# Experts of seven products: the products in another order, the gather issued an expert ahead, and the weight slots reloaded in another order

## The chip, the cores and the metric

The kernel runs on one core of a Trainium2 chip. The metric is the device time of one execution in microseconds, as a median over runs; the profile is of one further execution. Engines: PE (TensorE), DVE (VectorE), ACT (ScalarE), POOL (GpSimd), SP (SyncE, which here only issues DMAs).

## The reference, cut to what matters

A first block (attention, gated linear attention, RWKV branch) is followed by two layers, each a mixer and then a mixture of 16 experts. The change touches the two mixtures alone:

```python
def expert_choice_moe(x, w_router, w_gate_up, w_down):      # S = 1024, D = FF = 1024, 16 experts
    cap = CAPACITY_FACTOR * S // N_EXPERTS                  # 128 tokens an expert
    aff = jax.nn.softmax((x @ w_router), axis=-1)
    gates, idx = lax.top_k(jnp.swapaxes(aff, 1, 2), cap)
    xs = x[bi, idx]                                         # gather 128 rows
    g, u = jnp.split(jnp.einsum('becd,edf->becf', xs, w_gate_up), 2, axis=-1)
    out = jnp.einsum('becf,efd->becd', jax.nn.silu(g) * u, w_down) * gates[..., None]
    return jnp.zeros_like(x).at[bi, idx].add(out)           # scatter-add
```

An expert has 12 MB of fp32 weights (8 MB gate and up, 4 MB down), so the two mixtures read 400 MB of weights.

## The kernel before

`moe` handles the experts one after the other. Every engine has one instruction queue, worked in the order in which the program writes it, and semaphores tie the queues. The weights go through `ring`, 24 slots of 512 KB: slots 0 to 15 take gate and up, 16 to 23 take down. SP reloads a slot for the next expert when its readers are done.

Experts 0 to 2 and 15 multiply plainly. Experts 3 to 14 (`SEVEN`) compute gate and up, seen as a 2 x 2 block product (tokens halved by 64, rows of the weights halved, gate against up), by seven block products in the manner of Strassen and Winograd. Each quarter of the weights is 4 slots. In the names below a quarter is q0 to q3 (slots 0-3, 4-7, 8-11, 12-15).

- Sums of weights, on DVE, each over 128 x 1024 values and each in four parts j: t1 (in place in q1) = q1 - q0 (`sum_first`), t2 = q2 - t1 (`sum_second`), t3 = t2 - q0 (`sum_third`), t4 = t2 - q3, in place in t2 (`sum_fourth`).
- Sums of tokens, on POOL: s1, s3, s2, s4 in this order (`sum_tokens`, L4207 to L4212).
- Products, on PE, 16 matmul instructions each (L3631): 11 (q0), s2t2, s3t3, s1t1 (slots of q1), 22t4, 12b21 (q3), s4b22 (q2). `made` counts them in the order of `PRODUCTS`.
- Joins, on DVE, from PSUM banks (`join`): u2, u3, c22, u4, c21, 11, c12. The second half of the hidden row is sigmoid(c21) * c21 * c22, the first sigmoid(11) * 11 * c12; the sigmoids are ACT's.

PE's order for expert e is: s2t2, s3t3, s1t1, 22t4 | transposes of the next expert's gathered tokens (`turn_tokens`, L3604) | 12b21 | transposes of the second hidden half (`turn_half(e, 0)`, L3691) | s4b22 | first half of the next expert's product 11 | transposes of the first hidden half (`turn_half(e, 1)`) | second half of the next 11 | the down product, 32 matmul instructions (L3618). The last thing before `turn_half(e, 1)` is s4b22 -> c12 (L4067) -> product with the hidden half (L4070).

DVE's order is: u2, t4 parts 0 and 1, u3, t4 parts 2 and 3, c22, u4, c21 (L4049), c21 * c22 (L4051), product with the sigmoid (L4054), t1 parts 0 and 1 of the next expert (L4004), join 11 (L4059), t1 parts 2 and 3, product (L4065), c12, product (L4070), and then t2 and t3 of the next expert (L4012, L4016).

POOL's order is: gather of expert e+1 (L4195, an indirect DMA into `xg`, allowed once the tokens of e are transposed), token sums of e+1, scatter-add of e (L4232, after ACT has scaled the output). So the gather of e+1 stands behind the scatter of e-1.

SP's order of loads for e+1 is: slots 0-3 when t3 (all parts) and product 11 of e are made; slots 20-23 of e itself, four late slots; slots 4-7 after s1t1; 12-15 after 12b21; 8-11 after s4b22; 16-19 as the down product frees them.

Of the kernel before, what the change touches and what calls it, by code (L numbers as in the profile page):

```python
# [13 lines left out]
P = 128  # L14
# [3389 lines left out]
def moe(k, c, ps, io, layer, X, rows, out, sb):  # L3404
# [7 lines left out]
    with stage(k, sb) as st:  # L3412
# [39 lines left out]
        PRODUCTS = ("11", "s2t2", "s3t3", "s1t1", "22t4", "12b21", "s4b22")  # L3452
        JOINS = ("u2", "u3", "22", "u4", "21", "11", "12")
# [37 lines left out]
        quarter = lambda q, j: ring[:, 4 * q + j, :, :].rearrange("p x c -> p (x c)")  # L3491
        t2 = lambda j: X[:, j, :]
        t3 = lambda j: X[:, half_rows + j, :]

# [14 lines left out]
        def sync(sp):  # L3509
            def load(e, i):  # L3510
                sp.dma_start(ring[:, i, :, :], slab(e, i)).then_inc(*landed[i].up(16))

            for e in range(SEVEN[0] + 1):
                for i in range(SLABS if e < SEVEN[0] else 20):
                    if e:
                        sp.wait_ge(used.sem, used_at(e - 1, i + 1))
                    load(e, i)
                if e == 1:
                    sp.wait_ge(logits.sem, NT)
                    sp.dma_start(g, io["ln_ffn_g_2"][layer].partition_broadcast(P)).then_inc(*ln_in.up(16))  # L3520
                    sp.dma_start(b, io["ln_ffn_b_2"][layer].partition_broadcast(P)).then_inc(*ln_in.up(16))
            for e in SEVEN:
                sp.wait_ge(w_summed.sem, w_summed_at(e, "t3_3"))
                sp.wait_ge(made.sem, made_at(e, "11"))
                for i in range(4):
                    load(e + 1, i)
                for i in range(20, SLABS):
                    sp.wait_ge(used.sem, used_at(e - 1, i + 1))
                    load(e, i)
                sp.wait_ge(made.sem, made_at(e, "s1t1"))  # L3530
                for i in range(4, 8):
                    load(e + 1, i)
# [3 lines left out]
                sp.wait_ge(made.sem, made_at(e, "s4b22"))  # L3536
                for i in range(8, 12):
                    load(e + 1, i)
                for i in range(16, 20):
                    sp.wait_ge(used.sem, used_at(e, i + 1))  # L3540
                    load(e + 1, i)
            for i in range(20, SLABS):
                sp.wait_ge(used.sem, used_at(NE - 2, i + 1))
                load(NE - 1, i)
# [15 lines left out]
        def tensor(pe):  # L3560
# [54 lines left out]
            def multiply(e, i, lhsT, banks):  # L3615
                pe.wait_ge(landed[i].sem, 16 * (e + 1))
# [24 lines left out]
            def weight(q):  # L3641
                return lambda j: quarter(q, j)

            def landed_all(e, q):
                for j in range(4):
                    pe.wait_ge(landed[4 * q + j].sem, 16 * (e + 1))

            def first_product(e, lo, hi):

                if lo == 0:  # L3650
# [3 lines left out]
                    if e > SEVEN[0]:  # L3654
                        pe.wait_ge(joined.sem, joined_at(e - 1, "u3"))
                m = product(first_bank(e), x_quarter(e, 0, 0), weight(0), (lo, hi))
# [3 lines left out]
            def four_products(e):  # L3660
# [3 lines left out]
                pe.wait_ge(x_summed.sem, x_summed_at(e, "s2"))  # L3664
# [3 lines left out]
                product(ps[3], summed(0), weight(1)).then_inc(*made.up())  # L3668
# [3 lines left out]

            def fifth_product(e):

                pe.wait_ge(kept.sem, e - SEVEN[0] + 1)
                landed_all(e, 3)
                product(first_bank(e), x_quarter(e, 0, 1), weight(3)).then_inc(*made.up())

            def last_product(e):

                pe.wait_ge(joined.sem, joined_at(e, "u4"))
                pe.wait_ge(x_summed.sem, x_summed_at(e, "s4"))
                landed_all(e, 2)
                product(ps[3], summed(3), weight(2)).then_inc(*made.up())

            def turn_half(e, i):
# [3 lines left out]
                for b in range(4):  # L3690
                    m = pe.transpose(ps[4 + i][:, b * P:(b + 1) * P], hid[:, 512 * (1 - i) + b * P:512 * (1 - i) + (b + 1) * P],  # L3691
# [69 lines left out]
        def scalar(ac):  # L3761
# [43 lines left out]
            def keep_first(e):  # L3805

                if e > SEVEN[0]:
                    ac.wait_ge(acted.sem, 4 * e - 1)
# [3 lines left out]
            def sigmoid_half(e, i):  # L3812
                if i == 0:
                    ac.wait_ge(joined.sem, joined_at(e, "21"))
                    ac.activation(hid[:, 512:1024], c21, ACT.Sigmoid).then_inc(*sig.up())
                else:
                    ac.wait_ge(joined.sem, joined_at(e, "11"))
                    ac.activation(hid[:, 0:512], first_kept[:, :], ACT.Sigmoid).then_inc(*sig.up())

            def copy_half(e, i):  # L3820

                ac.wait_ge(h_turned.sem, 2 * e + i + 1)
                ac.activation(hs[:, :].rearrange("p (s b r t) -> p s b r t", s=2, b=4, r=2)[:, :, :, 1 - i, :],
# [28 lines left out]
            for e in range(NE - 1):  # L3852
                if e in SEVEN:
                    copy_tokens(e + 1)
                    for i in range(2):
                        sigmoid_half(e, i)
                        copy_half(e, i)
# [87 lines left out]
        def vector(ve):  # L3945
# [51 lines left out]
            def sum_first(e, j):  # L3997
# [4 lines left out]
                for q in (0, 1):  # L4002
                    ve.wait_ge(landed[4 * q + j].sem, 16 * (e + 1))
                ve.tensor_tensor(quarter(1, j), quarter(1, j), quarter(0, j), ALU.subtract).then_inc(*w_summed.up())  # L4004

            def sum_second(e, j):

                ve.wait_ge(landed[8 + j].sem, 16 * (e + 1))
# [3 lines left out]
                ve.tensor_tensor(t2(j), quarter(2, j), quarter(1, j), ALU.subtract).then_inc(*w_summed.up())  # L4012

            def sum_third(e, j):
                ve.wait_ge(w_summed.sem, w_summed_at(e, f"t2_{j}"))
                ve.tensor_tensor(t3(j), t2(j), quarter(0, j), ALU.subtract).then_inc(*w_summed.up())  # L4016

            def sum_fourth(e, j):

                ve.wait_ge(made.sem, made_at(e, "s2t2"))  # L4020
                ve.wait_ge(landed[12 + j].sem, 16 * (e + 1))
                ve.tensor_tensor(t2(j), t2(j), quarter(3, j), ALU.subtract).then_inc(*w_summed.up())  # L4022
# [8 lines left out]
            def join(e):  # L4031
# [11 lines left out]
                ve.wait_ge(made.sem, made_at(e, "s1t1"))  # L4043
                ve.wait_ge(joined.sem, joined_at(e, "u3"))
                ve.tensor_tensor(c22[:, :], ps[3][:, :], u3[:, :], ALU.add).then_inc(*joined.up())
                ve.wait_ge(made.sem, made_at(e, "s1t1"))
                ve.tensor_tensor(u2[:, :], ps[3][:, :], u2[:, :], ALU.add).then_inc(*joined.up())
# [4 lines left out]
                ve.wait_ge(sig.sem, 2 * e + 1)  # L4052
                ve.wait_ge(*acted.now())
                ve.tensor_tensor(hid[:, 512:1024], hid[:, 512:1024], c22[:, :], ALU.mult).then_inc(*acted.up())  # L4054
                if e + 1 in SEVEN:
                    sum_first(e + 1, 0)
                    sum_first(e + 1, 1)
                ve.wait_ge(made.sem, made_at(e, "12b21"))
                ve.tensor_tensor(first_kept[:, :], first_bank(e)[:, :], first_kept[:, :],  # L4059
                                 ALU.add).then_inc(*joined.up())  # L4060
                if e + 1 in SEVEN:
                    sum_first(e + 1, 2)
                    sum_first(e + 1, 3)
                ve.wait_ge(sig.sem, 2 * e + 2)
                ve.tensor_tensor(hid[:, 0:512], hid[:, 0:512], first_kept[:, :], ALU.mult).then_inc(*acted.up())  # L4065
                ve.wait_ge(made.sem, made_at(e, "s4b22"))
                ve.tensor_tensor(c12, ps[3][:, :], u2[:, :], ALU.add).then_inc(*joined.up())  # L4067
                ve.wait_ge(joined.sem, joined_at(e, "12"))
                ve.wait_ge(*acted.now())
                ve.tensor_tensor(hid[:, 0:512], hid[:, 0:512], c12, ALU.mult).then_inc(*acted.up())  # L4070
                if e + 1 in SEVEN:
# [121 lines left out]
        def gpsimd(gp):  # L4193
# [4 lines left out]
            def sum_tokens(e):  # L4198
# [6 lines left out]
                if e > SEVEN[0]:  # L4205
                    gp.wait_ge(made.sem, made_at(e - 1, "s4b22"))
# [160 lines left out]
```

## Time and profile before

| what | us |
|---|---|
| median of 3 runs | 4094.3 (4091.58 to 4097.19) |
| the profiled execution's own time | 4084.89 |
| its span | 4083.2 |
| PE busy | 3809.2 (93%) |
| DVE busy | 2042.4 (50%) |
| ACT busy | 1127.0 (28%) |
| POOL busy | 470.7 (12%) |
| granted share of PE's full clock, mean | 0.973 |

The two mixtures are the two stretches late in the span in which the 16 DMA engines are busy nine tenths of the time: about 2090 to 2850 and 3320 to 4083 us. Experts 3 to 14 fill 2279 to 2800 and 3510 to 4030 us of them.

### The profile page before, as it was taken

To read this page: it belongs to the slowest core of one execution; us is meant where nothing else is said; L and a number is where in the kernel's file an instruction comes from. 1 tells how busy PE (TensorE), PEld (TensorE's weight loads), DVE (VectorE), ACT (ScalarE), POOL (GpSimd) and SP (SyncE) were. 2 spreads that over 40 slices of the span, in tenths; PEclk is the share of its full clock that TensorE was granted. 3 is DMA by queue.
4 is the path that set the end of the run, shared out by engine and by line. 5 is a ranking of instruction groups with operands and counts; after the bars stand their busy time and mean duration, and the time that the engine had idled before them with its cause. 6 is when DMAs were issued, how large, how long until landed. Compare 5 with 4: busy or idle time off the path is not lost. (4 is left out here: it accounts for less than half of the span.)

```text
span 4083.2 us, 68182 instructions
## 1 busy us (share of the span) xinstructions
PE 3809.2 (93%) x28924; PEld 2006.4 (49%) x28924; DVE 2042.4 (50%) x3704; ACT 1127.0 (28%) x2409; POOL 470.7 (12%) x629
## 2 busy tenths in 40 slices
PE   8999999898989799999979999998999979999998
PEld 5555755757575644545544333333444444333333
DVE  2233334565656511146656566664366557566664
ACT  2343223434343301025531111113343421011113
POOL 3340002111111000000100111110000000111110
PEclk8998999999999999999989999999999989999999
DMA  4001101000100042020049899987211149899997
GB/s 107 27 26 39 33 27 47 9 22 9 27 4 22 4 143 78 11 62 1 1 181 325 298 322 314 315 316 275 74 37 31 52 170 320 282 324 319 326 325 255
DMA packets 271454, 567.51 MB, mean 139 GB/s; under 512 B 53504, under 2 KB 127392, under 8 KB 271152
## 3 DMA queue, kind: packets, MB, share of 16 engines
q1 hardware_dynamic: 255680, 506.01, 36.1%
q0 software_dynamic: 9504, 34.61, 3.2%
q10 hardware_dynamic: 5968, 22.55, 1.4%
q8 instruction: 229, 3.75, 0.4%
q14 instruction: 73, 0.60, 0.0%
HBM read 514.85 MB, written 48.23 MB: 138 GB/s over the span
## 5 line engine op out<-in xcount | busy, mean ns | idle before, releaser
L3618 PE MATMUL bank<-ring,m_hidden_T 128*128 128x512 f32 x1024 | 452.0, 597 | 0.0
L3618 PEld LDWEIGHTS bank<-ring,m_hidden_T 128*128 128x128 f32 x1024 | 192.4, 191 | 248.7 <-issue 248.7
L3618 PE MATMUL bank<-ring,m_picked_T 128*128 128x512 f32 x512 | 233.5, 614 | 4.1 <-ACT m_picked_T L3801 4.1
L1562 PE MATMUL bank<-hnT,first_block 128*128 128x336 f32 (+3 forms) x544 | 182.1, 487 | 8.0 <-PEq L101 7.3
L3631 PE MATMUL bank<-X,m_chosen 128*64 128x512 f32 x768 | 173.2, 604 | 6.3 <-POOL m_chosen L4210 6.3
L3631 PE MATMUL bank<-ring,m_chosen 128*64 128x512 f32 x768 | 174.2, 595 | 0.0
L4012 DVE TENSOR_TENSOR X<-ring 128x1024 f32<-128x1024 f32 x96 | 115.0, 1221 | 100.6 <-DMA ring<-in_moe_w_gate_up 99.7
L3618 PEld LDWEIGHTS bank<-ring,m_picked_T 128*128 128x128 f32 x512 | 99.3, 197 | 126.9 <-issue 121.5
L241 PE MATMUL bank<-xT,first_block 128*128 128x512 f32 x352 | 152.4, 593 | 2.8 <-ACT l_i L3269 1.7
L2825 PE MATMUL bank<-xT,a_weights 128*128 128x512 f32 x320 | 142.3, 595 | 0.8 <-ACT xT L2681 0.8
L1562 PEld LDWEIGHTS bank<-hnT,first_block 128*128 128x128 f32 x544 | 102.2, 193 | 66.0 <-issue 18.8
L2905 PE MATMUL bank<-a_weights,xT 128*128 128x512 f32 x256 | 126.7, 622 | 5.3 <-DMA a_weights<-in_attn_w_o 4.9
L484 PE MATMUL bank<-hnT,first_block 128*128 128x512 f32 (+3 forms) x336 | 119.2, 507 | 1.0 <-PEq L101 1.0
L484 PE MATMUL bank<-hnT,w_block 128*128 128x512 f32 (+3 forms) x304 | 119.5, 534 | 0.0
L4004 DVE TENSOR_TENSOR ring<-ring 128x1024 f32<-128x1024 f32 x96 | 113.3, 1218 | 3.0 <-DMA ring<-in_moe_w_gate_up 2.7
L3631 PEld LDWEIGHTS bank<-X,m_chosen 128*64 128x64 f32 x768 | 54.5, 139 | 122.3 <-issue 122.3
L1748 PE MATMUL bank<-rw_lane 64*64 64x64 f32 x2720 | 101.7, 220 | 12.7 <-issue 9.3
L1731 PE MATMUL bank<-rw_lane 64*64 64x64 f32 x2720 | 104.3, 221 | 9.8 <-issue 8.2
L3871 ACT ACTIVATE m_ys<-bank,m_gates 128x512 f32<-128x512 f32 x30 | 20.6, 687 | 336.0 <-PE bank L3618 336.0
L4016 DVE TENSOR_TENSOR X<-X,ring 128x1024 f32<-128x1024 f32 x96 | 113.0, 1218 | 0.0
L4022 DVE TENSOR_TENSOR X<-X,ring 128x1024 f32<-128x1024 f32 x96 | 112.8, 1217 | 0.0
L3221 PE MATMUL bank<-xT,l_gT 128*128 128x512 f32 x256 | 110.1, 592 | 0.8 <-ACT l_i L3269 0.8
(554 smaller groups left out, 7093.7 us busy)
## 6 DMA issues: line engine op xcount, KB each, us to landing
ring<-in_moe_w_gate_up SPq DMA_DIRECT2D x512, 512.0 KB, 7.5
ring<-in_moe_w_down SPq DMA_DIRECT2D x256, 512.0 KB, 5.6
first_block<-in_w_in SPq DMA_DIRECT2D x23, 512.0 KB, 3.9
w_block<-in_w_in SPq DMA_DIRECT2D x19, 512.0 KB, 3.9
x_rows<-X ACTq DMA_DIRECT2D x2, 4096.0 KB, 17.3
ring<-y_rows SPq DMA_DIRECT2D x16, 512.0 KB, 8.7
out_w<-in_w_out ACTq DMA_DIRECT2D x11, 512.0 KB, 12.3
first_block<-in_lru_w_in SPq DMA_DIRECT2D x11, 512.0 KB, 3.9
```

What stands on the lines that cost most here:

```text
L241: m = pe.matmul(ps[banks + j][0:out_rows, 0:n], w[:, d, 0:out_rows], src[:, d, col:col + n], start=d == 0, stop=d == KD - 1)
L484: x = pe.matmul(bank_of(s + j)[:, 0:w], wb[b % RING][:, d, :], hnT[:, d, col:col + w], start=d == 0, stop=d == KD - 1)
L1562: m = pe.matmul(banks[j][:, 0:n], wb[i % 3][:, d, :], hnT[:, d, col:col + n], start=d == 0, stop=d == KD - 1)
L2825: x = pe.matmul(main_bank(s)[:, :], w, xT[:, d, tokens_of(s)], start=d == 0, stop=d == KD - 1)
L2905: x = pe.matmul(ps[6 + half][:, :], oT[:, b, t * P:(t + 1) * P], weights[:, b, 512 * half:512 * half + 512], start=b == 0, stop=b == KD - 1)
L3221: out = pe.matmul(ps[2 * (t % 4) + h][:, :], gT[:, b, t * P:(t + 1) * P], wo[:, b, 512 * h:512 * h + 512], start=b == 0, stop=b == KD - 1)
L3618: m = pe.matmul(banks[j][:, :], lhsT[:, (i % 8) * P:(i % 8 + 1) * P], ring[:, i, j, :], start=i % 8 == 0, stop=i % 8 == KD - 1)
L3631: m = pe.matmul(bank[tok[half], :], tokens_(j), weights(j)[:, 512 * half:512 * half + 512], start=j == 0, stop=j == 3)
L4004: ve.tensor_tensor(quarter(1, j), quarter(1, j), quarter(0, j), ALU.subtract).then_inc(*w_summed.up())
L4012: ve.tensor_tensor(t2(j), quarter(2, j), quarter(1, j), ALU.subtract).then_inc(*w_summed.up())
L4016: ve.tensor_tensor(t3(j), t2(j), quarter(0, j), ALU.subtract).then_inc(*w_summed.up())
L4022: ve.tensor_tensor(t2(j), t2(j), quarter(3, j), ALU.subtract).then_inc(*w_summed.up())
```

## The change

The same seven products are made from the same sums. What moves:

- PE: s4b22, s2t2, s1t1, s3t3, 12b21 | transposes of the next tokens | 22t4 | transposes of the first hidden half | half of the next 11 | transposes of the second hidden half | other half of the next 11 | down. 22t4 is now last, and the hidden halves change places (half 0 first).
- DVE: the joins follow that order, with c22 = u2 + s1t1 first, c12 = c22 + s4b22, and s3t3 added to c22 afterwards; the number of joins and products stays. All four parts of t1 of the next expert now come after both hidden halves.
- POOL: from expert 3 on, the gather of e+2 is issued after the token sums of e+1, as soon as the tokens of e+1 have been transposed out of `xg`.
- ACT: sigmoid of half 0 before the copies of the next tokens, both sigmoids before the copies of the transposed halves.
- SP: slots 8-11 of e+1 after s4b22, 4-7 after s1t1, 12-15 after t4 and 12b21; slots 16-23 as the down product frees them, and between them slots 0 to 3 of e+2, one at a time, each when its part of t3 of e+1 is made.

```diff
-        PRODUCTS = ("11", "s2t2", "s3t3", "s1t1", "22t4", "12b21", "s4b22")
-        JOINS = ("u2", "u3", "22", "u4", "21", "11", "12")
+        PRODUCTS = ("11", "s4b22", "s2t2", "s1t1", "s3t3", "12b21", "22t4")
+        JOINS = ("u2", "u4", "12", "u3", "22", "11", "21")
...
+            for i in range(20, SLABS):
+                sp.wait_ge(used.sem, used_at(SEVEN[0] - 1, i + 1))
+                load(SEVEN[0], i)
+            sp.wait_ge(made.sem, made_at(SEVEN[0], "11"))
+            for i in range(4):
+                sp.wait_ge(w_summed.sem, w_summed_at(SEVEN[0], f"t3_{i}"))
+                load(SEVEN[0] + 1, i)
             for e in SEVEN:
-                sp.wait_ge(w_summed.sem, w_summed_at(e, "t3_3"))
-                sp.wait_ge(made.sem, made_at(e, "11"))
-                for i in range(4):
+                sp.wait_ge(w_summed.sem, w_summed_at(e, "t2_3"))
+                sp.wait_ge(made.sem, made_at(e, "s4b22"))
+                for i in range(8, 12):
                     load(e + 1, i)
-                for i in range(20, SLABS):
-                    sp.wait_ge(used.sem, used_at(e - 1, i + 1))
-                    load(e, i)
                 sp.wait_ge(made.sem, made_at(e, "s1t1"))
                 for i in range(4, 8):
                     load(e + 1, i)
+                sp.wait_ge(w_summed.sem, w_summed_at(e, "t4_3"))
                 sp.wait_ge(made.sem, made_at(e, "12b21"))
                 for i in range(12, 16):
                     load(e + 1, i)
...
+                for i in range(16, SLABS):
+                    if e + 2 < NE and i >= 20:
+                        sp.wait_ge(w_summed.sem, w_summed_at(e + 1, f"t3_{i - 20}"))
+                        sp.wait_ge(made.sem, made_at(e + 1, "11"))
+                        load(e + 2, i - 20)
                     sp.wait_ge(used.sem, used_at(e, i + 1))
                     load(e + 1, i)
...
+            def five_products(e):
+
+                pe.wait_ge(x_summed.sem, x_summed_at(e, "s4"))
+                landed_all(e, 2)
                 if e > SEVEN[0]:
                     pe.wait_ge(joined.sem, joined_at(e - 1, "21"))
+                product(ps[3], summed(3), weight(e, 2)).then_inc(*made.up())
                 pe.wait_ge(w_summed.sem, w_summed_at(e, "t2_3"))
                 product(ps[1], summed(2), t2).then_inc(*made.up())
+                pe.wait_ge(kept.sem, e - SEVEN[0] + 1)
+                product(first_bank(e), summed(0), weight(e, 1)).then_inc(*made.up())
                 pe.wait_ge(w_summed.sem, w_summed_at(e, "t3_3"))
                 product(third_bank(e), summed(1), t3).then_inc(*made.up())
+                pe.wait_ge(joined.sem, joined_at(e, "u4"))
+                landed_all(e, 3)
+                product(first_bank(e), x_quarter(e, 0, 1), weight(e, 3)).then_inc(*made.up())
...
-                    four_products(e)
+                    five_products(e)
                     turn_tokens(e + 1)
-                    fifth_product(e)
+                    last_product(e)
                     turn_half(e, 0)
-                    last_product(e)
                     ahead(e + 1, 0)
                     turn_half(e, 1)
                     ahead(e + 1, 1)
...
-                ve.wait_ge(made.sem, made_at(e, "s3t3"))
+                ve.wait_ge(made.sem, made_at(e, "s1t1"))
                 ve.wait_ge(joined.sem, joined_at(e, "u2"))
-                ve.tensor_tensor(u3[:, :], third_bank(e)[:, :], u2[:, :], ALU.add).then_inc(*joined.up())
+                ve.tensor_tensor(c22[:, :], first_bank(e)[:, :], u2[:, :], ALU.add).then_inc(*joined.up())
+                ve.wait_ge(joined.sem, joined_at(e, "u4"))
+                ve.tensor_tensor(c12, ps[3][:, :], c22[:, :], ALU.add).then_inc(*joined.up())
                 sum_fourth(e, 2)
                 sum_fourth(e, 3)
...
                 if e + 1 in SEVEN:
...
+                    for j in range(4):
+                        sum_first(e + 1, j)
                     sum_pairs(e + 1)
...
                 if e > SEVEN[0]:
-                    gp.wait_ge(made.sem, made_at(e - 1, "s4b22"))
+                    gp.wait_ge(made.sem, made_at(e - 1, "s3t3"))
...
             for e in range(NE - 1):
-                gp.wait_ge(x_turned.sem, e + 1)
-                gp.wait_ge(picked.sem, 2 * min(e + 2, FAST + 1))
-                gather(e + 1)
+                if e < SEVEN[0]:
+                    gp.wait_ge(x_turned.sem, e + 1)
+                    gp.wait_ge(picked.sem, 2 * min(e + 2, FAST + 1))
+                    gather(e + 1)
                 if e + 1 in SEVEN:
                     sum_tokens(e + 1)
+                    gp.wait_ge(x_turned.sem, e + 2)
+                    gather(e + 2)
                 gp.wait_ge(y_even.sem, e + 1)
```

## Rows read from the trace of the kernel before

**Rows 1.** Windows: experts 4 to 13 of each layer; busy us, clock, DMA share, GB/s.

```profile
2328.52:2755.60 427.08, 410.33 (x1602) 153.96 (x1601) 262.21 (x270) 52.89 (x90) 60.78 (x60) 1.00 0.91 319
3559.59:3984.98 425.39, 410.39 (x1602) 154.13 (x1601) 261.54 (x270) 52.89 (x90) 59.55 (x60) 1.00 0.92 321
```

**Rows 2.** Waits of PE in 2328.52:2755.60: us in total, times, longest.

```profile
PE bank L3691 <- DVE m_hidden L4070: 9.8, 10, 2.6
PE bank L3604 <- DMA m_picked<-x_rows,m_tokens: 7.0, 9, 1.3
```

**Rows 3.** Timeline of PE through one expert: start us, us, count, idle before.

```profile
2713.08 7.09 PE L3631 MATMUL bank<-X,m_chosen 128*64 128x512 f32 x32
2719.99 3.60 PE L3631 MATMUL bank<-ring,m_chosen 128*64 128x512 f32 x16
2723.43 3.60 PE L3631 MATMUL bank<-X,m_picked_T 128*64 128x512 f32 x16
2728.07 1.09 PE L3604 MATMUL bank<-ident,m_picked 128*128 128x128 f32 x8 [1.04 <-DMA m_picked<-x_rows,m_tokens]
2729.10 3.65 PE L3631 MATMUL bank<-ring,m_picked_T 128*64 128x512 f32 x16
2733.27 3.65 PE L3631 MATMUL bank<-ring,m_chosen 128*64 128x512 f32 x16
2736.75 1.89 PE L3631 MATMUL bank<-ring,m_spare 128*64 128x512 f32 x8
2739.24 0.63 PE L3691 MATMUL bank<-ident,m_hidden 128*128 128x128 f32 x4 [0.60 <-DVE m_hidden L4070]
2741.67 14.00 PE L3618 MATMUL bank<-ring,m_hidden_T 128*128 128x512 f32 x32
2755.60 1.94 PE L3631 MATMUL bank<-X,m_chosen 128*64 128x512 f32 x8
```

**Rows 4.** Timeline of PE: first products of expert 3, each layer.

```profile
2285.66 8.54 PE L3631 MATMUL bank<-X,m_chosen 128*64 128x512 f32 x32 [3.13 <-POOL m_chosen L4210]
3516.47 8.78 PE L3631 MATMUL bank<-X,m_chosen 128*64 128x512 f32 x32 [3.13 <-POOL m_chosen L4210]
```

**Rows 5.** Timeline of PE: token transposes under expert 14, each layer.

```profile
2770.48 1.09 PE L3604 MATMUL bank<-ident,m_picked 128*128 128x128 f32 x8 [0.93 <-DMA m_picked<-x_rows,m_tokens]
4000.08 1.09 PE L3604 MATMUL bank<-ident,m_picked 128*128 128x128 f32 x8 [1.15 <-DMA m_picked<-x_rows,m_tokens]
```

**Rows 6.** Groups of DVE in 2328.52:2755.60: busy, mean ns, idle before.

```profile
L4012 DVE TENSOR_TENSOR X<-ring 128x1024 f32<-128x1024 f32 x40 | 47.9, 1222 | 45.5 <-DMA ring<-in_moe_w_gate_up 45.1
L4070 DVE TENSOR_TENSOR m_hidden<-m_hidden,m_row 128x512 f32<-128x512 f32 x10 | 11.8, 1183 | 0.3
L4054 DVE TENSOR_TENSOR m_hidden<-m_hidden,m_junk 128x512 f32<-128x512 f32 x10 | 6.9, 693 | 19.9 <-ACT m_hidden L3815 19.9
```

**Rows 7.** Timeline of DVE and ACT in the same expert.

```profile
2727.08 0.69 DVE L4049 TENSOR_TENSOR m_row<-m_junk,bank 128x512 f32<-128x512 f32 x1 [2.15 <-PE bank L3631]
2733.72 0.68 DVE L4059 TENSOR_TENSOR m_junk<-bank,m_junk 128x512 f32<-128x512 f32 x1
2734.43 0.63 ACT L3818 ACTIVATE m_hidden<-m_junk 128x512 f32<-128x512 f32 x1 [0.46 <-DVE m_junk L4059]
2737.91 1.19 DVE L4070 TENSOR_TENSOR m_hidden<-m_hidden,m_row 128x512 f32<-128x512 f32 x1
```

**Rows 8.** Timeline of POOL: a token sum of expert 3, then of expert 14.

```profile
2276.78 7.37 POOL L4207 TENSOR_TENSOR m_chosen<-m_picked_T 128x256 f32<-128x256 f32 x1 [38.47 <-ACT m_picked_T L3803]
2737.11 0.75 POOL L4207 TENSOR_TENSOR m_chosen<-m_spare 128x256 f32<-128x256 f32 x1 [19.02 <-PE bank L3631]
```

**Rows 9.** DMA issues in 2328.52:2755.60: count, median us to landing.

```profile
ring<-in_moe_w_gate_up SPq DMA_DIRECT2D x159, 512.0 KB, 7.6
m_picked<-x_rows,m_tokens POOLq DMA_INDIRECT x10, 10.5
```

**Rows 10.** Windows: a burst of weight loads; PE after a longer idle time.

```profile
2545.70:2547.70 2.00, 2.00 (x12) 0.71 (x10) 2.00 (x2) 0.00 (x0) 0.38 (x1) 1.00 1.04 424
2569.70:2571.70 2.00, 2.00 (x8) 0.47 (x4) 0.00 (x0) 0.00 (x0) 0.00 (x0) 0.50 1.02 412
```

More of the change, by code:

```diff
@@ L3490, in moe, with landed_at @@
         c21, c12 = row0[:, 0:512], row0[:, 512:1024]
[L3491 removed]
+        quarter = lambda e, q, j: ring[:, 4 * q + j, :, :].rearrange("p x c -> p (x c)")
         t2 = lambda j: X[:, j, :]
         t3 = lambda j: X[:, half_rows + j, :]
+        def landed_at(e, i):
+            return landed[i].sem, 16 * (e + 1)
         def slab(e, i):
@@ L3639, in summed, with weight @@
                 return lambda j: x_sum(i)[:, j, :]
-            def weight(q):
-                return lambda j: quarter(q, j)
+            def weight(e, q):
+                return lambda j: quarter(e, q, j)
             def landed_all(e, q):
                 for j in range(4):
-                    pe.wait_ge(landed[4 * q + j].sem, 16 * (e + 1))
+                    pe.wait_ge(*landed_at(e, 4 * q + j))
             def first_product(e, lo, hi):
@@ L3671, in four_products @@
                 product(ps[1], x_quarter(e, 1, 1), t2).then_inc(*made.up())
[L3673 to L3684, printed above, removed]
             def turn_half(e, i):
@@ L3812, in sigmoid_half @@
             def sigmoid_half(e, i):
[L3813 to L3818, printed above, removed]
+                ac.wait_ge(joined.sem, joined_at(e, ("11", "21")[i]))
+                ac.activation(hid[:, 512 * i:512 * i + 512], (first_kept[:, :], c21)[i], ACT.Sigmoid).then_inc(*sig.up())
             def copy_half(e, i):
                 ac.wait_ge(h_turned.sem, 2 * e + i + 1)
-                ac.activation(hs[:, :].rearrange("p (s b r t) -> p s b r t", s=2, b=4, r=2)[:, :, :, 1 - i, :],
+                ac.activation(hs[:, :].rearrange("p (s b r t) -> p s b r t", s=2, b=4, r=2)[:, :, :, i, :],
                               ps[4 + i][:, :].rearrange("p (b s t) -> p s b t", b=4, s=2), ACT.Copy).then_inc(*h_even.up())
@@ L3853, in scalar @@
                 if e in SEVEN:
+                    sigmoid_half(e, 0)
                     copy_tokens(e + 1)
-                    for i in range(2):
-                        sigmoid_half(e, i)
-                        copy_half(e, i)
+                    sigmoid_half(e, 1)
+                    copy_half(e, 0)
+                    copy_half(e, 1)
                     if e + 1 in SEVEN:
@@ L4002, in sum_first @@
                 for q in (0, 1):
-                    ve.wait_ge(landed[4 * q + j].sem, 16 * (e + 1))
-                ve.tensor_tensor(quarter(1, j), quarter(1, j), quarter(0, j), ALU.subtract).then_inc(*w_summed.up())
+                    ve.wait_ge(*landed_at(e, 4 * q + j))
+                ve.tensor_tensor(quarter(e, 1, j), quarter(e, 1, j), quarter(e, 0, j), ALU.subtract).then_inc(*w_summed.up())
             def sum_second(e, j):
-                ve.wait_ge(landed[8 + j].sem, 16 * (e + 1))
+                ve.wait_ge(*landed_at(e, 8 + j))
                 ve.wait_ge(w_summed.sem, w_summed_at(e, f"t1_{j}"))
@@ L4037, in join @@
                 sum_fourth(e, 1)
-                ve.wait_ge(made.sem, made_at(e, "s3t3"))
+                ve.wait_ge(made.sem, made_at(e, "s1t1"))
                 ve.wait_ge(joined.sem, joined_at(e, "u2"))
-                ve.tensor_tensor(u3[:, :], third_bank(e)[:, :], u2[:, :], ALU.add).then_inc(*joined.up())
+                ve.tensor_tensor(c22[:, :], first_bank(e)[:, :], u2[:, :], ALU.add).then_inc(*joined.up())
+                ve.wait_ge(joined.sem, joined_at(e, "u4"))
+                ve.tensor_tensor(c12, ps[3][:, :], c22[:, :], ALU.add).then_inc(*joined.up())
                 sum_fourth(e, 2)
                 sum_fourth(e, 3)
[L4043 to L4047, printed above, removed]
+                ve.wait_ge(made.sem, made_at(e, "s3t3"))
+                ve.tensor_tensor(u3[:, :], third_bank(e)[:, :], u2[:, :], ALU.add).then_inc(*joined.up())
+                ve.tensor_tensor(c22[:, :], third_bank(e)[:, :], c22[:, :], ALU.add).then_inc(*joined.up())
+                ve.wait_ge(made.sem, made_at(e, "12b21"))
+                ve.tensor_tensor(first_kept[:, :], first_bank(e)[:, :], first_kept[:, :],
+                                 ALU.add).then_inc(*joined.up())
+                ve.wait_ge(joined.sem, joined_at(e, "11"))
+                ve.tensor_tensor(c12, c12, first_kept[:, :], ALU.mult).then_inc(*acted.up())
+                ve.wait_ge(sig.sem, 2 * e + 1)
+                ve.wait_ge(*acted.now())
+                ve.tensor_tensor(hid[:, 0:512], hid[:, 0:512], c12, ALU.mult).then_inc(*acted.up())
                 ve.wait_ge(made.sem, made_at(e, "22t4"))
@@ L4055, in join @@
                 if e + 1 in SEVEN:
[L4056 to L4071, printed above, removed]
+                    for j in range(4):
+                        sum_first(e + 1, j)
                     sum_pairs(e + 1)
```

31 lines of the change are left out of this document (11 added, 20 removed).

## The prediction

> **What bounds the kernel now.** I read the page first: one line of busy time says that PE works nearly always, and the 40 slices say that the weight-heavy mixtures also keep the DMA engines at nine tenths. So there are two candidates for the bound of experts 3 to 14, and the windows over ten whole experts of each layer separate them [rows 1]: an expert takes 42.71 us in layer one and 42.54 in layer two, PE is busy for 41.0 of it, DMA for 91 or 92% of it, DVE for 26.2. PE's own waits come next [rows 2]: it stands still for two things, the transposes of the second-finished hidden half, which wait for the product L4070 (9.8 us in ten experts), and the transposes of the gathered tokens, which wait for the gather (7.0 us). No wait for a weight load stands there. DVE does wait for weights, 4.5 us an expert, at t2 [rows 6], since q2 is loaded late, yet PE never waits for DVE's sums in these stretches. So PE is the bound with two small stalls an expert, and DMA is close behind.
>
> The timeline of PE through one expert turns this into a floor [rows 3]. Differences of starts: two products 6.91, a third 3.44, the fourth 4.64 of which 1.04 idle, token transposes 1.03, 12b21 and a set of hidden transposes 4.17, s4b22 3.48, half of the next product 2.49 of which 0.60 idle, transposes and other half 2.43, down 13.93. The sum is 42.52; without the two idle times 40.88.
>
> **The change part by part.** Let T be the moment at which token transposes can begin, so 12b21 has just ended.
>
> *PE.* The same instructions run, so the floor stays near 40.88. Five products now run in a row, so one change between transposes and products goes: 3.48 against 3.44 gives 0.04. s4b22 waits for more semaphores than the product that stood there, but the 12b21 of before waits for as many and shows no cost in its 4.17. I take 40.8 (bounds 40.7 and 41.0).
>
> *Gather.* Before, it is issued behind the scatter, a few us after an expert's first product began, and takes 10.5 us [rows 9]; the transposes come 15.0 us into the expert, so it is late by about 1. Now it is issued about 6 us after T, behind 3 to 4 us of token sums, and needed a whole period later: some 35 us for 10.5. Even if POOL were held through all 14.7 us of DVE's sums (12 at 1.222 [rows 6]), the gather would land near T + 32 of 40.8. The wait goes. Behind the gather on POOL stands only the scatter, not ready before the down product ends at about T + 23.5, so it isn't delayed. Both share POOL's DMA queue, now well apart. Saving 0.7 to 1.1 an expert.
>
> *The hidden half.* Before, s4b22 -> c12 -> L4070 -> transposes, covered by half a product; 0.60 was left over in the usual expert, 0.98 in the mean [rows 2, 3]. Now 22t4 -> c21 -> sigmoid -> product -> transposes: longer by a sigmoid, but covered by the first half's transposes too. In numbers from 22t4's end E: c21 starts at +0.1 (L4049 begins 0.2 after the 3.44 of 22t4 are over, against the 0.1 of a change to transposes) and takes 0.69; ACT follows 0.03 behind DVE and takes 0.63; DVE 0.04 behind that, 0.69 (L4054's mean); PE 0.14 behind DVE, as after L4070 [rows 3, 6, 7]. That is 2.32 to 2.38. The cover is 0.73 (4.17 less a product) less the 0.1 for the change, plus half a product, 1.89: 2.46 to 2.52. So nothing is left over, if DVE isn't slowed. What can slow it is POOL: L4070 runs beside token sums and takes 1183 ns against 693 for the same operation in L4054 [rows 6]. The new token sums begin when the tokens are copied: T + 1.0 for the transposes, two copies by ACT behind the first sigmoid, so T + 2.6; four sums at 0.75 [rows 8] end at T + 5.6. c21 * c22 starts at T + 5.4. They overlap by 0.2 and no more. Bounds: 0 left over, or 0.9 if both c21 * c22 and the product after it take 1.18. I take 0.05, nearest to the first. The sigmoid of half 0 ahead of the copies delays the copies by 0.35 at most; the product that needs them comes at T + 5.1, after T + 2.6. Half 0 itself is ready at T + 2.3 (join, sigmoid, product) and wanted at T + 4.6.
>
> *DVE's sums.* All of t1, t2 and t3 of the next expert now start at about T + 6.9, 12 x 1.222 = 14.7, done by T + 21.6; t2 is whole at T + 19.1. PE wants t2 at T + 27 (down ends at T + 23.5, then s4b22) and t3 at T + 34. Slack of 8 us, where before s2t2 came first and DVE's wait for q2 ate most of it. Under the products DVE fits as before: u2, two parts of t4, c22, c12, two parts of t4, u3, c22 sum to 4.9 for t4 and 3.4 for five joins, done 15.7 us after the expert begins, with t4 whole at 14.2 and wanted at 18.3. Price of losing the cover: one us for one.
>
> *Loads.* q2 is asked for after 3.4 us of the expert, q1 after 10.3, q3 after 17.2, the rest from T + 11 to T + 23.5. A slot takes 524 KB / 424 GB/s = 1.24 us in a burst [rows 10]; the largest batch, eight slots over the last four down steps, takes 10 us, with the scatter beside it 13. q2 of the next expert would be in by 12 us, wanted by DVE at 24; q1 by 17, wanted at 24; q3 by 24, wanted a whole expert later. SP's waits for t3 parts lie at T + 15.5 to T + 21.6, while the slots they stand before are freed at T + 18 to T + 23.5; the fourth delays nothing. So DVE's 4.5 us of waiting vanishes, and PE gains nothing from that, for it never waited there.
>
> *First and last expert.* Expert 3's first product after 11 was released by POOL's s2 and cost 3.13 idle, then a slower stretch: 8.36 for two products against 6.91, which fits a clock that falls after such an idle time: behind another one the granted clock is 0.50, the lower of its two levels, 1.2 GHz [rows 3, 4, 10]. Now s4 is needed, one sum later: 0.8 more, in each layer, and the same slow stretch. The long POOL sum there, 7.37 us [rows 8], lies beside DVE's weight sums. Expert 14 loses its wait for the gather, 0.93 and 1.15 [rows 5]; its hidden halves are covered anyway.
>
> Here the Trainium skill bears on the overlap (SBUF — State Buffer, "Who interferes with whom"): a DVE instruction with both inputs in SBUF contends with a GpSimd instruction that reads SBUF, and the one that starts second waits for the other's end. The trace agrees: 1183 against 693 ns, and 7.37 us for one token sum against 0.75. By that rule alone DVE could lose at most what is left of one token sum, twice, and the sum would be B's below rather than the forecast's.
>
> **Sum.** Period 40.85. Layer one, ten experts: 427.08 - 408.5 = 18.6. Layer two: 425.39 - 408.5 = 16.9. Expert 3 in each: 42.9 and 43.1 before, 42.3 now, and 0.8 lost ahead of it: nothing. Expert 14: 2.1. Together 37.6; I drop the fraction, 37. On the profiled execution that is 4084.9 to 4048; the runs' median lies 9.4 above that execution, and I subtract the same 37 from it: **4057**.
>
> **The rivals.**
>
> *Forecast, 72%:* both stalls go, 4050 to 4065. The upper end has 0.3 us left over at the hidden half.
>
> *B, the hidden half still stalls, 14%.* POOL's sums fall on both DVE operations: 0.9 an expert, 22 of them, 20 us: 4077. For: POOL's sums took up to 1.18 where they met DVE, which would lengthen them to T + 7. Against: DVE is idle from T + 2.3 to T + 4.7, so they meet nothing.
>
> *C, no change, 5%.* Idle times that the engine's records don't name (switching, waits per semaphore, clock) fill the place: 4088 to 4100. For: PE waits on six semaphores before s4b22. Against: [rows 3] shows such switches at 0.1 to 0.2.
>
> *D, slower: DMA becomes the bound with a hole in it, 8%.* The DMA engines' share times the period is 38.9 us an expert. If that work doesn't shrink, and SP asks for nothing between q3's landing (T + 5) and the first freed down slot (T + 11.2), the period is 38.9 + 6.2 = 45.1, 2.5 over today's: 22 times is 55 us, 4149. It decides as soon as the hole is over 3.7 us, what 42.6 leaves. For: 91% is near full. Against: the gather now falls into that hole, and the share counts engines as busy at 319 GB/s that carry 424 in a burst, so the work shrinks when it is bunched: 24 slots are 30 us, the indirect transfers some 4.
>
> *E, more than forecast, 1%:* under 4045, if the expert 3 stalls went too.
>
> **How the numbers follow.** The time is the forecast's. 8 in 10: from 4047, a few us below the forecast's end for the runs' own scatter of 5.6, to 4078, which takes in B. Faster or slower by 0.2% (8 us, what this kernel's runs can tell): faster is forecast, B and E, 0.87; same 0.05; slower 0.08.
>
> **What would show it.** Right: the windows over ten experts at 408 to 412; no PE wait for the gather; the transposes behind 22t4 within 0.3; DVE's wait at t2 gone; DVE's busy time per expert unchanged or a little lower; DMA share up to 0.95. Wrong: PE waiting for a weight load or for a t2 or t3 part (D), L4070's successor at 1.18 with a PE wait behind it (B), or a period over 41.5 with no named wait (C).

## The result: faster by 0.9%, and the profile after

Four runs of the changed kernel have a median of 4051.7 us (4050.35 to 4055.84), four of the kernel before 4092.9 (4088.44 to 4097.19). The ratio is 0.9907, 95% interval 0.9889 to 0.9925: 31 to 45 us less. The forecast was 4057. The profiled execution took 4050.4 us against 4084.9.

The windows over ten experts of each layer, in the columns of [rows 1], begin at the down product of expert 3 this time:

```profile
2318.31:2725.97 407.66, 407.66 (x1602) 153.79 (x1600) 255.81 (x271) 51.81 (x90) 57.85 (x60) 1.00 0.92 335
3528.87:3936.53 407.66, 407.66 (x1602) 153.79 (x1600) 255.82 (x271) 51.80 (x90) 57.78 (x60) 1.00 0.92 335
```

PE's busy time equals the window in both layers. An expert takes 40.77 us, all of them the same, and the view of PE's waits is empty there, where [rows 2] had 16.8 us for ten experts. Timeline of PE through one expert, against [rows 3]:

```profile
2699.14 3.65 PE L3637 MATMUL bank<-ring,m_chosen 128*64 128x512 f32 x16
2712.92 3.60 PE L3637 MATMUL bank<-ring,m_picked_T 128*64 128x512 f32 x16
2716.46 1.09 PE L3610 MATMUL bank<-ident,m_picked 128*128 128x128 f32 x8
2717.48 3.65 PE L3637 MATMUL bank<-X,m_picked_T 128*64 128x512 f32 x16
2721.06 0.66 PE L3694 MATMUL bank<-ident,m_hidden 128*128 128x128 f32 x4
2721.65 1.94 PE L3637 MATMUL bank<-ring,m_spare 128*64 128x512 f32 x8
2723.53 0.64 PE L3694 MATMUL bank<-ident,m_hidden 128*128 128x128 f32 x4
2724.11 1.94 PE L3637 MATMUL bank<-ring,m_spare 128*64 128x512 f32 x8
2725.97 14.00 PE L3624 MATMUL bank<-ring,m_hidden_T 128*128 128x512 f32 x32
```

The token transposes come 17.3 us into the expert without a wait, and the second set of hidden transposes 1.88 us after the half product's start, where 2.49 stood. Groups of DVE and issues of DMA in the first window, against [rows 6, 9]:

```profile
L4011 DVE TENSOR_TENSOR X<-ring 128x1024 f32<-128x1024 f32 x40 | 47.1, 1218 | 0.0
L4054 DVE TENSOR_TENSOR m_hidden<-m_hidden,m_row 128x512 f32<-128x512 f32 x10 | 6.9, 692 | 1.0
L4061 DVE TENSOR_TENSOR m_hidden<-m_hidden,m_junk 128x512 f32<-128x512 f32 x10 | 6.9, 692 | 1.0
```

```profile
ring<-in_moe_w_gate_up SPq DMA_DIRECT2D x160, 512.0 KB, 9.6
m_picked<-x_rows,m_tokens POOLq DMA_INDIRECT x10, 5.8
```

DVE no longer waits for weights at t2 (45.5 us before), both products with a hidden half take 0.69, and the gather lands in 5.8 us instead of 10.5, away from the scatter.

At the two ends of a layer PE still stops. Timeline of PE and POOL under expert 3, against [rows 4, 8]:

```profile
2289.77 5.35 PE L3637 MATMUL bank<-ring,m_chosen 128*64 128x512 f32 x16 [3.84 <-POOL m_chosen L4205]
2280.18 7.37 POOL L4200 TENSOR_TENSOR m_chosen<-m_picked_T 128x256 f32<-128x256 f32 x1 [39.72 <-ACT m_picked_T L3805]
```

Under expert 14 the gather's wait of [rows 5] is gone, but PE loses 0.48 us there (1.07 from the start of the first hidden transposes to the next multiplication instead of 0.59). Its wait is for c21 (L4056): expert 15 multiplies into a bank that c21 still reads.

### The profile page after: what moved, and what is told of

Same layout as the page of the kernel before. It is cut to its first block and busy times, and to the rows that moved or that the text cites. A ratio compares the mean times of both kernels' runs of the same rounds, so it can differ in the third digit from the quotient of the medians.

```text
span 4048.5 us, 68222 instructions
## 1 busy us (share of the span) xinstructions
PE 3801.2 (94%) x28924; PEld 2003.7 (49%) x28924; DVE 2028.9 (50%) x3704; ACT 1124.9 (28%) x2409; POOL 466.3 (12%) x629
## 5 line engine op out<-in xcount | busy, mean ns | idle before, releaser
L4034 DVE TENSOR_TENSOR m_junk<-bank,m_junk 128x512 f32<-128x512 f32 x24 | 16.6, 692 | 243.7 <-PE bank L3637 243.7
L3816 ACT ACTIVATE m_hidden<-m_junk 128x512 f32<-128x512 f32 x24 | 15.2, 632 | 416.6 <-DVE m_junk L4048 416.6
L3637 PEld LDWEIGHTS bank<-ring,m_chosen 128*64 128x64 f32 x768 | 54.0, 139 | 125.4 <-issue 115.9
```

The lines of the kernel that those rows point to most:

```text
L3637: m = pe.matmul(bank[tok[half], :], tokens_(j), weights(j)[:, 512 * half:512 * half + 512], start=j == 0, stop=j == 3)
```

## The experiments

The kernels below that start with "before" are the old kernel with single parts of the change put in; those with "after" are the changed kernel with single parts taken out or put in. Medians of different chips are not compared; each ratio is to the kernel before on the same chip. The ten-expert windows of the two layers (from down to down) leave out the stages ahead of the experts, which differ by up to 17 us from profile to profile: product 11 of expert 3 starts at 2278.9 in the profile of before, 2282.3 in the changed one, 2280.1 in the same kernel once more, 2271.5 in before_t1_alone and 2288.4 in before_late_sums, though nothing ahead of it was edited. Each window is one execution, though, and where PE's stalls vary from expert to expert it is no finer than the ratio. By the same cut the kernel before has 427.1 and 425.4, the changed one 407.7 twice.

**before_early_gather**: POOL's part of the change alone.

```diff
-                gp.wait_ge(x_turned.sem, e + 1)
-                gp.wait_ge(picked.sem, 2 * min(e + 2, FAST + 1))
-                gather(e + 1)
+                if e < SEVEN[0]:
+                    gp.wait_ge(x_turned.sem, e + 1)
+                    gp.wait_ge(picked.sem, 2 * min(e + 2, FAST + 1))
+                    gather(e + 1)
                 if e + 1 in SEVEN:
                     sum_tokens(e + 1)
+                    gp.wait_ge(x_turned.sem, e + 2)
+                    gather(e + 2)
```

> The kernel before with POOL's part of the change alone: from expert 3 on the gather of e+2 is issued after the token sums of e+1. My theory (PE is the bound and stalls at two places, one of them the gather): the wait of the token transposes goes, the ten-expert windows shrink from 427 and 425 to about 417 and 416 us, 20 to 24 us less in all (4069 to 4073 against 4093); the wait for L4070 stays at 0.6 us or more an expert. Rival (DVE's waits for weight loads are what the change removed, the gather was a symptom): the window stays within 2 us of before, as the idle time moves to another wait.

Ratio 0.9966 (0.9955 to 0.9978), windows 418.6 and 424.6. The gather's wait is gone everywhere, but the hidden half's grew: 10 waits, 14.9 us, in the second layer. The gain is 14 us, not 20. Timeline of DVE and PE in one of its long stalls:

```profile
3742.33 2.50 DVE L4004 TENSOR_TENSOR ring<-ring 128x1024 f32<-128x1024 f32 x2 [0.67 <-DMA ring<-in_moe_w_gate_up]
3744.74 0.68 DVE L4059 TENSOR_TENSOR m_junk<-bank,m_junk 128x512 f32<-128x512 f32 x1
3745.34 2.35 DVE L4004 TENSOR_TENSOR ring<-ring 128x1024 f32<-128x1024 f32 x2
3747.61 1.22 DVE L4065 TENSOR_TENSOR m_hidden<-m_hidden,m_junk 128x512 f32<-128x512 f32 x1
3748.75 0.68 DVE L4067 TENSOR_TENSOR m_row<-bank,m_junk 128x512 f32<-128x512 f32 x1
3749.47 1.18 DVE L4070 TENSOR_TENSOR m_hidden<-m_hidden,m_row 128x512 f32<-128x512 f32 x1
3750.79 0.63 PE L3691 MATMUL bank<-ident,m_hidden 128*128 128x128 f32 x4 [2.03 <-DVE m_hidden L4070]
3751.35 1.94 PE L3631 MATMUL bank<-ring,m_picked_T 128*64 128x512 f32 x8
```

s4b22 ends at 3746.9. c12 could start then, but stands behind two pairs of t1, the first of which waited for its weights, and starts at 3748.75. A late load reaches PE through DVE's queue, though no row names a wait of PE for it. It is not the load alone: against the expert of [rows 7] (its rows stand below, under before_gather_t1) c12 is 1.43 us later after s4b22, 0.89 of it because t1 is later and 0.54 because L4065 takes 1.22 instead of 0.68, beside token sums.

**before_late_sums**: one line in `sum_tokens` of the old kernel, `gp.wait_ge(acted.sem, 4 * e)`.

> The kernel before with one more wait: POOL's token sums of e+1 start only when both hidden halves of e are done, so they no longer run beside c12 and the product L4070. My theory (the hidden half stalls because POOL's sums slow the DVE operation, 1183 against 693 ns): L4070 takes 0.69, PE's wait for it falls from 0.98 to 0.1 to 0.4 an expert, 11 to 18 us less in all. Rival (the chain is simply too long for its cover): L4070 is faster, but PE waits nearly as long, under 4 us less in all. A second rival: the sums now meet t2 and t3 on DVE and delay s2, which the first product of the next expert needs; then PE waits for POOL and the time is not lower.

Ratio 0.9982 (0.9966 to 0.9998), windows 427.1 and 421.5. L4070 takes 0.69 when POOL is out of its way, and 13 of the 20 experts stop there for under 0.2 us. In the others the half product still takes 2.3 to 4.4 us, where t1 was late. In the first window that wait falls from 9.8 to 5.0 us, but the one for the gather grows from 7.0 to 9.5, and two of the products behind it take 5.3 us instead of 3.6. So POOL's sums were only part of that stall.

**after_old_gather** (the reverse of the diff above, in the changed kernel) and **after_old_loads** (SP's loads in the old order, the wait for t4 kept; the lines left out load 4-7 after s1t1, 12-15 after t4 and 12b21, then 8-11, then 16-19 as they are used):

```diff
             for e in SEVEN:
-                sp.wait_ge(w_summed.sem, w_summed_at(e, "t2_3"))
-                sp.wait_ge(made.sem, made_at(e, "s4b22"))
-                for i in range(8, 12):
+                sp.wait_ge(w_summed.sem, w_summed_at(e, "t3_3"))
+                sp.wait_ge(made.sem, made_at(e, "11"))
+                for i in range(4):
                     load(e + 1, i)
+                for i in range(20, SLABS):
+                    sp.wait_ge(used.sem, used_at(e - 1, i + 1))
+                    load(e, i)
...
```

> The changed kernel with the gather where it was, behind the scatter. The new product order alone puts the token transposes 17.3 us into an expert instead of 13.8, and the gather, issued 4 us into it, lands 10.5 to 12 us later, at 14.5 to 16. My theory now: the gather's early issue is not needed beside the new order, the period stays 40.8 and the time is within 3 us of the changed kernel (4052). Rival (what I reckoned in the prediction as the gather's saving belongs to its early issue): the wait comes back, 0.7 to 1.1 an expert, 16 to 24 us more, 4068 to 4076.

> The changed kernel with SP's loads in nearly the old order: slots 0-3 after all of t3, then the late slots 20-23 of the same expert, then 4-7, 12-15 and only then 8-11, 16-19. My theory (PE does not wait for weights in either order; DVE's sums have 8 us of slack before t2 is wanted): DVE may wait at t2 again, PE does not, period 40.8, time within 3 us of the changed kernel (4052). Rival (the load order carries part of the gain): PE waits for a load or for a t2 part, period 41.5 or more, 16 us or more above the changed kernel.

Ratios 0.9907 (0.9875 to 0.9938) and 0.9906 (0.9881 to 0.9931), the changed kernel's. Their windows, first layer each:

```profile
2316.05:2723.72 407.67, 407.67 (x1602) 153.80 (x1601) 255.84 (x271) 51.75 (x90) 53.89 (x60) 1.00 0.91 335
```

```profile
2317.92:2725.58 407.66, 407.66 (x1602) 153.79 (x1600) 257.32 (x271) 51.76 (x90) 57.82 (x60) 1.00 0.93 335
```

With the old gather it again takes 10.4 us, but lands before 17.3. With the old loads DVE waits at t2 again, and PE does not notice:

```profile
DVE X L4008 <- DMA ring<-in_moe_w_gate_up: 16.1, 13, 3.1
```

**after_again**, **after_order_alone** (both edits above together), **after_long_chain** and **after_yield** ran on one chip.

> The changed kernel itself once more, beside the three that follow, so that they can be compared with it on the same chip: 4048 to 4056, period 40.77. How far its stages ahead of the experts differ from those of its first profile shows what a single profile's total can tell.

Ratio 0.9912 (0.9898 to 0.9927), period 40.77.

> The changed kernel with both the gather and SP's loads in the old places, so the new order of products, joins and hidden halves alone. Each of the two undone by itself cost nothing. My theory: both together cost nothing either, period 40.77, time as after_again within 3 us. Rival (each covers for the other: old loads put slots 20-23 and the scatter beside the late gather, so it lands after 17.3 us): the transposes wait, 0.3 to 1 us an expert, 7 to 24 us more.

Ratio 0.9917 (0.9902 to 0.9932), 4047.8 against 4047.0 for the changed kernel beside it, period 40.77. The order of products and of DVE's and ACT's work is enough; gather and loads add nothing to it. That order includes the new place of t1, behind both hidden halves. No run has the new products with t1 in its old place, so what the order of the products gives the hidden half by itself stays open.

```diff
                 ve.wait_ge(made.sem, made_at(e, "22t4"))
+                ve.tensor_tensor(u2[:, :], u3[:, :], ps[1][:, :], ALU.subtract)
                 ve.tensor_tensor(c21, u3[:, :], ps[1][:, :], ALU.subtract).then_inc(*joined.up())
```

> The changed kernel with one DVE operation of 0.69 us more between 22t4 and c21, in every expert of SEVEN (it writes u2, which nobody reads any more). It measures the cover of the last hidden half. My theory (chain 2.38 against 2.46 to 2.52 of cover): 0.08 to 0.14 of it is hidden and PE waits 0.55 to 0.6 us an expert, period 41.3 to 41.4, 12 to 14 us more in all. Rival (there is more slack than I reckoned): under 0.3 an expert, under 7 us more. Rival on the other side (the added operation pushes the next ones under POOL's sums or its gather, and the idle time lowers the clock): over 1 us an expert, over 24 us more.

4061.6 against 4047.0, windows 413.5 twice: 0.59 us an expert for an operation of 0.69. So 0.10 of cover was left, as reckoned.

```diff
                     sum_second(e, j)
                     sum_second(e, j + 1)
+                    if e == SEVEN[0] and j == 0:
+                        ve.wait_ge(x_summed.sem, x_summed_at(e, "s4"))
```

> The changed kernel with one wait more on DVE, in expert 3 alone: after the first two parts of t2 DVE waits until POOL has made s4. My theory (PE's stall of 4.06 us ahead of s4b22 of expert 3 is POOL held off by DVE's sums, 7.37 us for one token sum, and the slow product behind it, 5.18 against 3.49, is the clock that fell in the stall): POOL's four sums take 0.72 each, PE does not stop, s4b22 takes 3.49, 5.7 us less in each layer, 11 us less in all, about 4041. Rival (DVE's lost 3 us are missing elsewhere: t2 comes after PE wants it, or the scaled output of expert 2 comes late): PE waits there instead, 0 to 4 us less in all.

4038.7 against 4047.0, ratio to before 0.9892 (0.9876 to 0.9907). Timeline of DVE, POOL and PE in expert 3:

```profile
2277.64 0.72 POOL L4202 TENSOR_TENSOR m_chosen<-m_picked_T 128x256 f32<-128x256 f32 x1 [39.19 <-ACT m_picked_T L3805]
2280.56 2.36 DVE L4015 TENSOR_TENSOR X<-X,ring 128x1024 f32<-128x1024 f32 x2 [2.95 <-POOL m_chosen L4207]
2283.21 3.60 PE L3637 MATMUL bank<-ring,m_chosen 128*64 128x512 f32 x16
2286.65 3.60 PE L3637 MATMUL bank<-X,m_chosen 128*64 128x512 f32 x16
```

A token sum takes 0.72 instead of 7.37, DVE gives up 2.95 us, and PE runs s4b22 straight after product 11 (2279.73) and s2t2 behind it. The gain is 8 us of the 11 forecast.

**before_gather_t1** and **before_all_three**: the old kernel, old order of products, with the early gather and t1 moved; the second with the late token sums too.

```diff
-                if e + 1 in SEVEN:
-                    sum_first(e + 1, 0)
-                    sum_first(e + 1, 1)
                 ve.wait_ge(made.sem, made_at(e, "12b21"))
...
-                if e + 1 in SEVEN:
-                    sum_first(e + 1, 2)
-                    sum_first(e + 1, 3)
...
                 if e + 1 in SEVEN:
+                    for j in range(4):
+                        sum_first(e + 1, j)
                     sum_pairs(e + 1)
```

> The kernel before with the early gather and with all four parts of t1 of the next expert behind both hidden halves on DVE, instead of two and two between their operations. In before_early_gather the stall at the first hidden half was 0.61 in most experts but 2.0 to 2.2 in eight, where DVE had waited for q1 to land with c12 queued behind it. My theory: the long stalls go, the stall is 0.6 in every expert, period 41.42 throughout, about 12 us less than before_early_gather, 4060 to 4066. Rival (the long stalls come from POOL, not from the loads): they stay. A second rival: t1 now starts later, t2 comes after s2t2 wants it, and PE waits there.

> before_gather_t1 with POOL's token sums after both hidden halves as well, so the old order of products with three stalls taken away one by one. My theory (three causes make up the whole of the change's gain, and the order of the products is only the means): L4070 at 0.69, stall at 0.1, period 40.85 to 40.95, within 4 us of the changed kernel. Rival (the product order gives something of its own, as DVE's t2 sums would now run beside POOL's or s2 would be late): period over 41.2.

Ratios 0.9915 (0.9897 to 0.9932) and 0.9908 (0.989 to 0.9926); the second has 407.7 in both windows too. Windows of the first:

```profile
2311.47:2719.14 407.67, 407.67 (x1603) 153.77 (x1601) 273.57 (x271) 51.82 (x90) 84.97 (x61) 1.00 0.93 335
3523.47:3931.14 407.67, 407.67 (x1602) 153.79 (x1601) 273.13 (x271) 51.88 (x90) 85.04 (x61) 1.00 0.94 335
```

The old order of products reaches the same 40.77. The 0.6 us that I expected to stay are gone too, without the third edit. Timeline of DVE, POOL and PE there, and, below, the rows of the kernel before that lead to L4070 of [rows 7]:

```profile
2715.08 0.69 DVE L4061 TENSOR_TENSOR m_row<-bank,m_junk 128x512 f32<-128x512 f32 x1 [1.76 <-PE bank L3631]
2715.81 0.69 DVE L4064 TENSOR_TENSOR m_hidden<-m_hidden,m_row 128x512 f32<-128x512 f32 x1
2715.92 1.17 POOL L4204 TENSOR_TENSOR m_chosen<-m_spare 128x256 f32<-128x256 f32 x1
2716.68 0.66 PE L3691 MATMUL bank<-ident,m_hidden 128*128 128x128 f32 x4
```

```profile
2736.59 0.68 DVE L4065 TENSOR_TENSOR m_hidden<-m_hidden,m_junk 128x512 f32<-128x512 f32 x1
2737.19 0.68 DVE L4067 TENSOR_TENSOR m_row<-bank,m_junk 128x512 f32<-128x512 f32 x1
2737.82 0.73 POOL L4208 TENSOR_TENSOR m_chosen<-m_spare 128x256 f32<-128x256 f32 x1
```

In the kernel before, c12 stood behind t1 and began 0.2 us late; L4070 then began at 2737.91, 0.09 after a token sum, and took 1.19. Here c12 starts at once, the product begins 0.11 ahead of a token sum, takes 0.69, and the token sum takes 1.17.

**before_t1_alone** and **before_gather_t1_yield** (with `x_summed_at(e, "s2")` in the wait of after_yield).

> The kernel before with the move of t1 behind both hidden halves alone; gather, loads and products as before. before_gather_t1 showed both stalls gone and the whole gain there. My theory (two causes, each with its own wait): the stall at the hidden half goes (first half of the next product 1.82 instead of 2.49 to 4.5), the wait for the gather stays at 0.8 to 1.1 an expert; period 41.6 to 41.9, about 19 us over before_gather_t1 in the profile's 24 experts, 4060 to 4066. Rival (the gather was late only because the loads, held up by a stalled PE, ran beside it): it lands in time now as well, period 40.8.

Ratio 0.9963 (0.9947 to 0.9979), windows 423.1 and 415.7. No stall at the hidden half, ten waits for the gather in each window (11.4 and 7.3 us), and behind the two longest, 1.97 and 2.22 us, the next product was slow:

```profile
2502.41 1.09 PE L3604 MATMUL bank<-ident,m_picked 128*128 128x128 f32 x8 [1.97 <-DMA m_picked<-x_rows,m_tokens]
2503.43 5.35 PE L3631 MATMUL bank<-ring,m_spare 128*64 128x512 f32 x16
```

> before_gather_t1 with DVE waiting in expert 3 for POOL's s2 after the first two parts of t2, as after_yield does for s4. The old order wants s2 and all of t2 right after product 11, the changed order has s4b22 in between. My theory: PE still waits 1 to 1.5 us for t2 there, without a drop of the clock, 4 us less in each layer than before_gather_t1, about 4037 to 4041, level with after_yield (ratio to before 0.989 to 0.991). Rival (the new order earns its place at this start): PE waits over 2.5 us for t2, the clock falls again, no gain on before_gather_t1.

Ratio 0.9891 (0.9872 to 0.991), level with after_yield's 0.9892; these two are the fastest that ran. PE waits 1.8 us for t2 (5.25 between two starts, less the 3.44 of a product), without a slow product behind it:

```profile
2280.78 7.09 PE L3631 MATMUL bank<-X,m_chosen 128*64 128x512 f32 x32 [1.59 <-DVE X L4012]
```

## Why the prediction was right, and where its reasons were not

- *PE is the bound, the floor is 40.8:* right, 40.77. DMA at 92 to 94% of the time was no bound; rival D did not appear in any order of loads.
- *The gather:* the saving came, but the step I named for it, the early issue, was not needed. after_old_gather keeps the late issue and has no wait: the gather is issued 4.0 us into the expert and lands 10.4 later, and the new order alone puts the transposes at 17.3 us instead of 13.9 + 1. The prediction has that moment (17.2, under the loads), and I did not hold it against the gather. In the old order the early issue does remove the wait (before_early_gather).
- *The hidden half:* 0.05 left over forecast; measured, 1.88 against the 1.82 of a half product that nothing delays (before_gather_t1, 2714.86 to 2716.68). The margin of 0.08 to 0.14 was measured as 0.10. For the kernel before, however, I blamed POOL's sums and the chain. before_gather_t1 shows the head of the cause: t1 on DVE in front of c12. It cost 0.2 us in the usual expert and pushed L4070 behind a token sum; where q1 landed late, the stall was about 2 us, token sums having their part in it.
- *"PE gains nothing from DVE's waits, for it never waited there"* is the sentence that failed. It holds for q2 (after_old_loads), not for q1, whose wait PE saw under L4070's name.
- *What was enough:* two different sets of edits reach 40.77, the new orders of PE, DVE and ACT without the early gather (after_order_alone), and the early gather with t1 moved in the old order (before_gather_t1). The move of t1 is in both.
- *The sum:* 37 forecast; the two profiles differ by 34.5, the medians by 41, after_again's by 35. The two ten-expert stretches gave 37.2 (427.1 + 425.4 - 815.3, from down to down). Ahead of s4b22 expert 3 went as said: 7.49 - 6.78 = 0.71 more. But "the same slow stretch" is not one size: s4b22 took 5.18 us in layer one and 6.41 in layer two, so expert 3 lost 0.3 and 1.3 us, not nothing. Expert 14 gained 0.7 and 0.9 instead of 2.1 together: its new 0.48 was missed ("its hidden halves are covered anyway"), and the bank, not the cover, decides there. The remaining 2.7 us between 37.2 and 34.5 lie in stages that no edit touched.
- *One reading of the code was off:* the 12b21 of before waits on five semaphores, not on six. The s4b22 of before does wait on six, so the conclusion stands.
- *How the parts add:* over both layers, the ten-expert windows lose 9.2 us by the early gather alone, 13.8 by t1 alone, and 37.1 by both. These are single executions; by the ratios the three are 14 us (9 to 18), 15 (9 to 22) and 35 (28 to 42), so that the whole is more than its parts is likely but not clear of noise. What the windows show is that one stall can grow when the other goes: the hidden half's from 7.7 to 14.9 us in layer two of before_early_gather, the gather's from 7.0 to 11.4 in layer one of before_t1_alone. In the other layer of each they went from 9.8 to 8.9 and stayed at 7.3.

## What to carry to other kernels

A wait is named after the last link of its chain. When a stall varies from one round to the next (0.6, then 2.0), look at what stands in front of that link in its engine's queue and at what that waited for, before the link's own duration is blamed.

When a loop has two stalls, price them together: removing either gave 14 or 15 us by the ratios, removing both 35, and in two of four windows one stall had grown when the other was gone. And when every stall is gone, look at the loop's first round: one wait that made DVE yield to POOL gave 8 us more.

## What the runs showed of the hardware

A DVE operation with two SBUF inputs and a POOL sum that meet: in the rows above, whoever started first kept its time and the other one waited (DVE took 1.19 when it began 0.09 us after POOL, and 0.69 when it began 0.11 us ahead). The Trainium skill says so (SBUF — State Buffer, "Who interferes with whom"). In expert 3, against six DVE sums in a row (t2 and t3, L4012 and L4016), a single POOL sum took 7.37 us, ten times its 0.72, so the wait was not for one operation's end there: POOL got no turn between them until they ended. That is not so for every run of DVE sums. Beside t1's four in before_gather_t1 the two engines took turns, and both got slower, DVE from 1.22 to 1.61 us a sum and POOL to 1.59 to 1.70:

```profile
L4004 DVE TENSOR_TENSOR ring<-ring 128x1024 f32<-128x1024 f32 x41 | 63.9, 1614 | 0.0
L4206 POOL TENSOR_TENSOR m_chosen<-m_chosen,m_spare 128x256 f32<-128x256 f32 x5 | 8.5, 1704 | 0.0
```

What decides between the two cases no run here shows. PE did not see the slower t1 sums, as the period stayed at 40.77.

PE's clock: the length of a wait alone did not decide whether it fell. Over all runs PE stood 16 times for 1.7 to 2.7 us in experts 3 to 14. Behind eight of these waits the next products were slower: the 5.35 us above instead of 3.6 (granted clock 0.68 in it), or 3.39 for half a product instead of 1.87 behind 2.63 us in the kernel before (granted clock 0.54, about the lower of the two levels, 1.2 GHz). Behind the other eight they were not, as with the 1.94 behind 2.03 us in before_early_gather (granted clock 1.00). None of seven waits of 1.4 to 1.6 us was followed by a slow product, and each of the 3.1 and 3.8 us ahead of expert 3's second product was. The slow s4b22 behind the latter was 1.7 us longer than a product in one layer of the changed kernel and 3.0 in the other (5.18 and 6.41).
